# Router weights loaded early, the sample tile projected on four strips of the array, and cache pages gathered in 8 KB rows by GpSimd

## The chip, the cores and the metric

The kernel runs on one core of a Trainium2 chip. A core has a matrix engine (TensorE, PE in the rows; its weight loads are PEld), VectorE (DVE), ScalarE (ACT), GpSimd (POOL) and SyncE (SP), which only issues transfers here. SP, ACT and POOL each have a queue of DMA issues; all of them run on the same 16 DMA engines. The metric is device microseconds (us) from start to end, as the median of several executions. All data is float32.

## The reference, cut to what matters

One decoder layer is computed for 512 prompt tokens and for 8 sample sequences of 4 new tokens (32 tokens), with shared weights:

```
h            = rms_norm(x) @ w_in                      # 1024 -> q,k,v (512 each), hq,f,i,g (512 each), 2 gates (1024 each)
o_sb prompt  = stick-breaking attention over 512 tokens, 8 heads of 64
o_sb sample  = the same over 4096 cached rows per sequence: cache_k[page_table], cache_v[page_table]
               page_table (8, 32) picks pages of 128 rows; a row is 8 heads x 64 floats = 2 KB
o_hg         = HGRN2 recurrence (prompt in chunks; 8 sample states of 64x64 per head are read and written)
x           += (sigmoid(ga) * (o_sb @ w_a) + sigmoid(gb) * (y_b @ w_b)) @ w_out
h2           = rms_norm(x); router: h2 @ w_group (4), h2 @ w_expert (32); top group, top 2 experts of it
x           += sum of weight * expert(h2)              # 32 experts, SwiGLU, 3 matrices of 2 MB each
```

## The kernel before

Each engine has its own program, and semaphores order them. The stages, in TensorE's order, are these.

**Projections and prompt attention (0 to 342 us).** The input projection runs in seven chunks of 512 columns, q, k, v, hq, f, i and g, each a 2 MB weight load. Chunks q, k, hq and g are kept transposed ("cols"). Chunks v, f and i are kept with tokens on the partitions ("rows"): five jobs each, four of 128 prompt rows and a fifth of the 32 sample rows (`project`, L641: 8 steps of the inner dimension, each with 512 moving columns; float32 products appear as two instructions each). ScalarE copies a job out of PSUM (`projection_out`, L1226). q, k and v are projected first (13 jobs), then two jobs of hq. The other jobs are interleaved with the 8 heads of the prompt attention: one between a head's scores (L683) and its remain sums (L693, L697), and one between the remain sums and the next head's scores (two before the remain sums of head 0). The fifth job of f comes after the remain sums of head 2, and the fifth job of i before the remain sums of head 5. ScalarE's and VectorE's softplus chain runs while the first of the two jobs does (ScalarE L1260 to L1266, VectorE L1532 to L1578 for the losses, L1580 to L1583 for the arguments). Before head 0 ScalarE issues one transfer, `lb_logits`.

**Page loop (342 to 754 us).** There are 64 units; a unit is 4 pages of one sequence, 1 MB of keys and 1 MB of values. For unit n TensorE transposes two pages (L766), computes the scores of unit n-1 (L777), transposes the other two, and from n = 7 on (`LAG`) sums the values of unit n-7 (L799). ScalarE (L1338) and VectorE (L1744) copy the transposed keys out of PSUM. After each fourth unit the softplus chain of a set runs on ScalarE and VectorE, and `turn_weights` (L788) transposes the result. From unit 4 to unit 52 every second unit is followed by a part of the HGRN2 recurrence (L821 to L917). Keys and values have rings of three buffers each. The small sample-to-sample products (L736 to L752, `new_rows` semaphore) are placed among the first units.

SP issues the cache loads, one DMA for a page: 128 partitions, 2 KB each (`key_loads` L355, `value_loads` L363). It reads the page numbers into registers first. Its order is keys of n, then values of n-6:

```
for n in range(2, UNITS + LAG - 1):
    if n < UNITS:
        key_loads(n)          # waits: pages of unit n-3 turned
    if n == LAG - 1:
        sp.wait_ge(S("rows_stored"), 64)
        sp.wait_ge(S("new_rows"), 4)
    if n >= LAG - 1:
        value_loads(n - LAG + 1)   # waits: values of unit n-9 summed
```

The weights of the first two branch products (`gate_loads(0)`, 2 MB in 1 KB runs) are issued near the end of this loop at n = 67; `w_branch_a`, `w_branch_b` and `gate_loads(1)` follow after the loop. GpSimd loads the sample states (L530, 16 DMAs), and stores them (L538) when they are done.

**End of the loop (712 to 754 us).** After the scores of unit 63 TensorE sums the values of units 57 to 59, turns the last weights, does `branch_product(0, 0)` (L943), sums units 60 and 61, does `branch_product(0, 1)`, and sums units 62 and 63.

**Branch products (754 to 917 us)**: L943 for the gates and L946 for the two branches.

**Mixing and router (917 to 1020 us).** TensorE multiplies with `w_out`, first the samples (L998: 32 stationary columns, four strips of the output at once), then four prompt tiles (L1005). Between them it transposes the rows (L1019) and computes router logits (`router`, L1031). VectorE first clears a scratch area (L1813) and the router weights (L1814). ScalarE waits for that (`route_zero`), issues the five loads of router weights and biases (L1194) and loads its function table (L1402). VectorE multiplies the router weights with `norm2_w` (L1901) before the first `router`.

**Experts (1020 to 1500 us).** SP streams 6 MB per expert through three buffers. The weights of expert 2 are issued when mixing is done and, in part, when the first gather of rows has landed. GpSimd gathers token rows with an indirect DMA (`rows_in`, L559) and scatters the results (`rows_out`, L567). Then the results are added and stored (until 1520 us).

## Time and profile before

| | us |
|---|---|
| median of 3 runs | 1527.18 (1525.68 to 1533.15) |
| profiled execution, its own time | 1522.24 |
| its span, first to last instruction | 1520.5 |
| TensorE busy | 1339.0 (88%) |
| VectorE, ScalarE, GpSimd busy | 394.6, 353.0, 87.3 |

The profile is of one execution. "Busy" of TensorE includes the fill of its pipeline, so 88% is not 88% of its peak. "PEclk" is the clock granted to TensorE as a share of 2.4 GHz, averaged over a stretch (1.00 is 2.4 GHz, 0.50 is 1.2 GHz). "DMA share" is the mean busy share of the 16 DMA engines; it reads a little over 1 in some stretches. An entry such as `[1.30 <-DMA arena<-in_cache_k]` behind an instruction says that its engine stood idle for 1.30 us before it and what ended that.

### The profile page before, as it was taken

The page shows a single profiled execution, that of the slowest core. Times are in us where ns is not written, and L with a number is a line of the kernel's source. Part 1 is how long each engine was busy: PE and PEld are TensorE (multiplying, and loading weights), DVE is VectorE, ACT ScalarE, POOL GpSimd, SP SyncE. Part 2 cuts the span into 40 slices and gives each one's busy share as a digit, 9 for nine tenths or more (in the row PEclk, how much of TensorE's full clock was granted, in tenths as well). Part 3 has the DMA queues.
Part 4 walks back from the last instruction along what each step waited for, and adds up shares of the span by engine and source line. Part 5 has one row for each costly group of instructions (what it writes and reads, how often), then busy time and mean ns, then how long its engine had stood idle before and what let it go on. Part 6 is the DMA issues. An engine that isn't in the chain of part 4 may idle for free.

```text
span 1520.5 us, 22239 instructions
## 1 busy us (share of the span) xinstructions
PE 1339.0 (88%) x8780; PEld 797.2 (52%) x8780; DVE 394.6 (26%) x723; ACT 353.0 (23%) x566; POOL 87.3 (6%) x144
## 2 busy tenths in 40 slices
PE   7999999978999999787799997969988887888873
PEld 5847544555666667555688883544333332333331
DVE  2012343443444444342011102341111111011103
ACT  2023242424444443564000001110100000000000
POOL 3000000011000000200000000010110101001000
PEclk9999999998999999999899998979999898899987
DMA  6113200018999998999781105049999999999995
GB/s 225 56 56 128 83 0 0 0 45 242 334 358 378 348 344 314 386 383 352 279 321 56 56 25 205 28 158 412 425 426 426 426 426 425 426 426 425 427 392 193
DMA packets 119640, 395.94 MB, mean 260 GB/s; under 512 B 17075, under 2 KB 25284, under 8 KB 107250
## 3 DMA queue, kind: packets, MB, share of 16 engines
q1 hardware_dynamic: 109506, 380.41, 64.5%
q0 software_dynamic: 5984, 11.18, 2.2%
q10 hardware_dynamic: 4048, 2.93, 0.6%
q8 instruction: 71, 1.16, 0.3%
q14 instruction: 31, 0.25, 0.0%
HBM read 386.06 MB, written 16.27 MB: 265 GB/s over the span
## 4 chain that ended last, share of the span: by engine, by line
PE 71%; issue 7%; DVE 6%; DMA 5%; SPq 5%; ACT 4%; ACTq 1%; POOLq 0%; DVEq 0%
PE ps L1118 16%; PE ps L943 8%; PE ps L1141 7%; PE ps L638 7%; PE ps L766 5%; PE ps L641 5%; PE ps L946 4%; PE ps L1005 3%; DMA arena<-in_cache_k 3%; PE ps L777 3%; SPq L363 2%; PE ps L799 2%; SPq L355 2%; PE ps L1129 1%; PE ps L693 1%
## 5 line engine op out<-in xcount | busy, mean ns | idle before, releaser
L1118 PE MATMUL ps<-arena 128*64 128x512 f32 x512 | 252.9, 652 | 68.2 <-issue 66.8
L1119 PE MATMUL ps<-arena 128*64 128x512 f32 x512 | 253.4, 653 | 0.0
L1118 PEld LDWEIGHTS ps<-arena 128*64 128x64 f32 x512 | 74.0, 150 | 212.8 <-issue 210.6
L766 PE MATMUL ps<-ident,arena 128*128 128x128 f32 x1024 | 149.5, 292 | 27.4 <-DMA arena<-in_cache_k 21.4
L766 PEld LDWEIGHTS ps<-ident,arena 128*128 128x128 f32 x1024 | 118.0, 148 | 99.1 <-issue 68.9
L1338 ACT ACTIVATE arena<-ps 128x512 f32<-128x512 f32 x192 | 108.5, 595 | 173.6 <-PE ps L766 173.6
L943 PE MATMUL ps<-mixers,arena 128*128 128x272 f32 x512 | 120.7, 397 | 6.8 <-DMA arena<-in_w_in 6.8
L638 PE MATMUL ps<-mixers,arena 128*128 128x272 f32 x512 | 120.4, 397 | 0.5 <-DVE mixers L1491 0.5
L943 PEld LDWEIGHTS ps<-mixers,arena 128*128 128x128 f32 x512 | 98.2, 192 | 27.8 <-DMA arena<-in_w_in 7.2
L638 PEld LDWEIGHTS ps<-mixers,arena 128*128 128x128 f32 x512 | 97.8, 192 | 21.1 <-DVE mixers L1491 0.6
L641 PE MATMUL ps<-arena,mixers 128*128 128x512 f32 (+1 forms) x240 | 105.4, 594 | 0.0
L1744 DVE COPY arena<-ps 128x512 f32<-128x512 f32 x64 | 44.2, 690 | 178.6 <-PE ps L766 178.5
L1141 PE MATMUL ps<-arena,attn_masks 128*64 128x512 f32 x176 | 81.4, 606 | 0.5 <-DVE attn_masks L1990 0.5
L1142 PE MATMUL ps<-arena,attn_masks 128*64 128x512 f32 x176 | 81.4, 606 | 0.0
L777 PE MATMUL ps<-arena 128*32 128x512 f32 x512 | 75.6, 665 | 0.0
L1119 PEld LDWEIGHTS ps<-arena 128*64 128x64 f32 x512 | 74.0, 150 | 0.0
L799 PE MATMUL ps<-arena 128*32 128x128 f32 x2048 | 69.6, 278 | 3.2 <-DMA arena<-in_cache_v 3.1
L641 PEld LDWEIGHTS ps<-arena,mixers 128*128 128x128 f32 (+1 forms) x240 | 40.9, 174 | 56.6 <-issue 55.8
L1965 DVE TENSOR_TENSOR arena<-ps,arena 128x1024 f32<-128x1024 f32 x16 | 19.6, 1225 | 187.9 <-PE ps L1104 187.7
L799 PEld LDWEIGHTS ps<-arena 128*32 128x32 f32 x2048 | 52.8, 110 | 14.8 <-issue 10.9
L946 PE MATMUL ps<-mixers,arena 128*128 128x272 f32 x256 | 59.8, 392 | 0.0
L1005 PE MATMUL ps<-arena 128*128 128x512 f32 x128 | 59.7, 617 | 0.0
(333 smaller groups left out, 1355.3 us busy)
## 6 DMA issues: line engine op xcount, KB each, us to landing
arena<-in_cache_k SPq DMA_DIRECT2D x256, 256.0 KB, 5.0
arena<-in_cache_v SPq DMA_DIRECT2D x256, 256.0 KB, 5.0
arena<-in_w_gate_exp SPq DMA_DIRECT2D x32, 2048.0 KB, 32.2
arena<-in_w_up_exp SPq DMA_DIRECT2D x32, 2048.0 KB, 37.0
arena<-in_w_down_exp SPq DMA_DIRECT2D x22, 2048.0 KB, 37.7
mixers<-in_w_down_exp SPq DMA_DIRECT2D x10, 2048.0 KB, 37.4
arena<-in_w_in SPq DMA_DIRECT2D x7, 2048.0 KB, 8.6
arena<-in_w_in SPq DMA_DIRECT2D x8, 1024.0 KB, 14.2
```

Source lines behind the costliest of these rows:

```text
L638: last = mm(ps[:, bank + hf, 0:TH], wring[:, c % 3, k, P * j:P * j + P], hT[:, k, TH * hf:TH * hf + TH], start=k == 0, stop=k == KD - 1)
L641: last = mm(ps[0:ROWS[j], bank, :], hT[:, k, P * j:P * j + ROWS[j]], wring[:, c % 3, k, :], start=k == 0, stop=k == KD - 1)
L766: last = turn(ps[:, TURN + j % 2, P * c:P * c + P], kring[n % 3][:, j, P * c:P * c + P], ident[:, :])
L777: last = mm(ps[32 * c:32 * c + 32, ZB, :], qblk_of(m // NGRP, s, c), d_kt[:, n % 2, c, :], start=s == 0, stop=s == PER_SET - 1)
L799: last = mm(ps[32 * c:32 * c + 32, VB, P * s:P * s + P], d_at[:, m % 2, j, 32 * c:32 * c + 32], vring[:, n % 3, j, P * c:P * c + P], start ...
L943: last = mm(ps[:, bank + hf, 0:TH], gw[m // 2 % 2][e][:, k, P * (m % 2):P * (m % 2) + P], hT[:, k, cols], start=k == 0, stop=k == KD - 1)
L946: last = mm(ps[:, bank + hf, 0:TH], wab[e - 2][:, k, P * m:P * m + P], (osbT, ybT)[e - 2][:, k, cols], start=k == 0, stop=k == CT - 1)
L1005: last = mm(ps[:, 2 * (p % 2) + hf, :], mrg[:, k, P * i:P * i + P], wo[k][:, 512 * hf:512 * hf + 512], start=k == 0, stop=k == KD - 1)
L1118: mm(ps[0:BLK, 1 + u, :], own, wgv[w][:, k, :], start=k == 0, stop=k == KD - 1)
L1119: last = mm(ps[BLK:P, 1 + u, :], own, wuv[w][:, k, :], start=k == 0, stop=k == KD - 1)
L1141: mm(ps[0:BLK, 5 + u, :], m_h[:, u, j, :], wdv[w][:, j, 0:512], start=j == 0, stop=j == FJ - 1)
L1338: fn(d_kt[:, n % 2, :, P * j:P * j + P], each(ps[:, TURN + j % 2, :], CT), ACT.Copy).then_inc(S("kT_act"), 1)
```

## The change

There are three parts.

**Router weights.** The five loads of router weights and biases are issued by ScalarE before the attention of head 0, ahead of `lb_logits`, into a tensor of their own that GpSimd clears at the start. `route_zero` no longer stands ahead of them. VectorE's memset of the weights goes.

**Sample tile.** The fifth job of the chunks v, f and i is computed as four matmuls per step instead of one, each with the same 32 stationary columns and 128 of the 512 moving columns, into four strips of 32 output partitions. ScalarE copies the four strips out with four instructions.

**Pages.** GpSimd issues one indirect DMA for the keys of a unit and one for its values. Each partition gets 8 KB, four adjacent rows of a page. The row numbers of all 64 units are computed at the start by VectorE from the page table, which is broadcast to all partitions. Position n of the loop now holds the keys of n and then the values of n-7. The wait for `new_rows` stands before the keys of unit 4; the values of units 0, 1 and 2 are issued at positions 4, 5 and 6. SP is left with the state loads and stores, and issues `gate_loads(0)` and `gate_loads(1)` as soon as the recurrence is done and the branch weights when unit 63 is scored. ScalarE reads and writes the scores of a set in another order of columns (two instructions per set, with a stride), since a buffer's columns no longer follow the order of the cache rows.

```diff
@@ TensorE, project
+                    elif j < 4:
+                        last = mm(ps[:, bank, :], hT[:, k, P * j:P * j + P], wring[:, c % 3, k, :],
+                                  start=k == 0, stop=k == KD - 1)
                     else:
-                        last = mm(ps[0:ROWS[j], bank, :], hT[:, k, P * j:P * j + ROWS[j]], wring[:, c % 3, k, :],
-                                  start=k == 0, stop=k == KD - 1)
+                        for q in range(4):
+                            last = mm(ps[32 * q:32 * q + TS, bank, 0:P], hT[:, k, SEQ:T], wring[:, c % 3, k, P * q:P * q + P],
+                                      start=k == 0, stop=k == KD - 1)
@@ ScalarE, projection_out
+                        for q in range(4):
+                            last = fn(dst[0:TS, j, P * q:P * q + P], ps[32 * q:32 * q + TS, bank, 0:P], func, scale=scale)
@@ GpSimd
+            def unit_loads(n, out, rows, landed):
+                pool.indirect_dma_start(
+                    out=flat(out), out_offset=None, in_=rows,
+                    in_offset=bass.IndirectOffsetOnAxis(ap=unit_i[:, n:n + 1].bitcast(U32), axis=0),
+                    bounds_check=LAST_ROW, oob_is_err=False).then_inc(S(f"{landed}_{n % 3}"), 16)
+            def key_loads(n):
+                if n >= 3:
+                    pool.wait_ge(S("page_turned"), GP * (n - 2))
+                unit_loads(n, kring[n % 3], k_rows, "cache_k")
+            def value_loads(n):
+                if n >= 3:
+                    pool.wait_ge(S("values_summed"), n - 2)
+                unit_loads(n, vring[:, n % 3], v_rows, "cache_v")
+            pool.wait_ge(S("unit_rows"), 1)
+            pool.wait_ge(S("heads_normed"), 2 * CT)
+            key_loads(0)
+            pool.wait_ge(S("attn_weights"), H)
+            key_loads(1)
+            key_loads(2)
             pool.wait_ge(S("attn_values"), H)
             nc.gpsimd.memset(flat(state[:, 0]), 0.0).then_inc(S("states_zero"), 1)
+            key_loads(3)
+            pool.wait_ge(S("rows_stored"), 64)
+            pool.wait_ge(S("new_rows"), 4)
+            for n in range(4, UNITS + LAG):
+                if n < UNITS:
+                    key_loads(n)
+                if n in (4, 5, 6):
+                    value_loads(n - 4)
+                elif n >= LAG + 3:
+                    value_loads(n - LAG)
@@ SP (state loads and stores moved here from GpSimd; cache loads gone)
+            sp.wait_ge(S("yb"), 1)
+            gate_loads(0)
+            gate_loads(1)
             sp.wait_ge(S("unit_scores"), UNITS)
             for e in range(2):
                 sp.dma_start(wab[e], w_br[e]).then_inc(S("w_branches"), 16)
-            gate_loads(1)
@@ ScalarE, order of columns, and router loads moved ahead of lb_logits
-                fn(d_z, ps[:, ZB, :], ACT.Identity, scale=SCALE, bias=d_c[:, 0:1])
+                fn(d_z.rearrange("p (q r) -> p q r", r=GP), ps[:, ZB, :].rearrange("p (r q) -> p q r", r=GP), ACT.Identity, ...)
-            act.wait_ge(S("route_zero"), 1)
-            load(w2c, ...); load(wr[:, :, 0:NG], ...); load(wr[:, :, 8:8 + NE], ...); load(r_b ...) x2
```

## Rows read from the trace of the kernel before

**Rows 1.** The page: span, and busy time of TensorE.

```profile
span 1520.5 us, 22239 instructions
PE 1339.0 (88%) x8780; PEld 797.2 (52%) x8780; DVE 394.6 (26%) x723; ACT 353.0 (23%) x566; POOL 87.3 (6%) x144
```

**Rows 2.** Busy time by stretch, then clock, DMA share and GB/s.

```profile
372.00:600.00 228.00, 222.53 (x3048) 156.80 (x3049) 99.24 (x178) 105.61 (x187) 1.25 (x2) 0.94 0.97 346
...
615.70:711.70 96.00, 77.55 (x988) 51.28 (x988) 34.24 (x47) 54.32 (x87) 9.96 (x16) 0.98 1.05 384
...
753.70:917.00 163.30, 161.72 (x712) 133.72 (x714) 18.73 (x32) 8.72 (x14) 0.00 (x0) 1.00 0.37 131
...
1040.00:1480.00 440.00, 373.17 (x1662) 146.75 (x1663) 53.18 (x84) 35.04 (x59) 43.97 (x44) 0.91 1.01 424
```

**Rows 3.** Waits: from 600 to 715 us, then from 372 to 600 us.

```profile
PE ps L766 <- DMA arena<-in_cache_k: 18.0, 15, 3.8
...
PEld ps L766 <- DMA arena<-in_cache_k: 5.2, 7, 1.5
```

**Rows 4.** Timeline of TensorE, unit 56: start, duration, instructions, idle before.

```profile
673.00 1.09 PE L766 MATMUL ps<-ident,arena 128*128 128x128 f32 x8 [1.30 <-DMA arena<-in_cache_k]
...
676.04 1.08 PE L799 MATMUL ps<-arena 128*32 128x128 f32 x32
678.63 1.09 PE L766 MATMUL ps<-ident,arena 128*128 128x128 f32 x8 [1.51 <-DMA arena<-in_cache_k]
```

**Rows 5.** DMA queues: packets, MB, share of 16 engines' span.

```profile
q1 hardware_dynamic: 109506, 380.41, 64.5%
q0 software_dynamic: 5984, 11.18, 2.2%
```

**Rows 6.** The chain that ended last: start, us, what.

```profile
83.40 34.45 PE ps L641 x80
...
210.03 6.98 PE ps L641 x16
```

**Rows 7.** Timeline: the arguments of head 2, and the strips of L998.

```profile
212.07 0.28 DVE L1583 TENSOR_TENSOR arena<-arena,attn_masks 128x128 f32<-128x128 f32 x1
...
916.75 3.66 PE L998 MATMUL ps<-arena 128*32 128x256 f32 x64 [1.57 <-DVE arena L1811]
```

**Rows 8.** Timeline: head 0, losses done and remain sums begun.

```profile
152.72 0.28 DVE L1578 TENSOR_TENSOR arena<-arena,mask_lt 128x128 f32<-128x128 f32 x1
...
157.63 1.02 PE L693 MATMUL ps<-arena,attn_masks 128*128 128x512 f32 x2
```

**Rows 9.** Timeline: the first units.

```profile
361.46 0.42 DVE L1638 COPY arena<-ps 128x256 f32<-128x256 f32 x1 [0.34 <-PE ps L752]
...
364.81 1.10 PE L766 MATMUL ps<-ident,arena 128*128 128x128 f32 x8 [0.34 <-ACT arena L1338]
```

**Rows 10.** GpSimd's gathers of token rows (tile view).

```profile
L559 POOL DMA_INDIRECT arena<-expert_rows,load_i x16: 988/1042/1190, 1014.5 to 1403.1; - x16
...
DMA to landing us min/median/max: 4.1/12.5/13.2
```

**Rows 11.** Timeline of TensorE at the end of the page loop.

```profile
721.98 1.93 PE L799 MATMUL ps<-arena 128*32 128x128 f32 x32 [3.12 <-DMA arena<-in_cache_v]
723.85 1.12 PE L788 MATMUL ps<-ident,arena 128*128 128x128 f32 x4
731.76 9.31 PE L943 MATMUL ps<-mixers,arena 128*128 128x272 f32 x32 [6.79 <-DMA arena<-in_w_in]
```

**Rows 12.** Timeline around the first router product.

```profile
920.86 4.17 ACTq L1194 DMA_DIRECT2D mixers<-in_w_expert_router  x1
...
925.07 8.37 ACTq L1194 DMA_DIRECT2D arena<-in_b_group_router  x1
...
937.79 1.27 PE L1031 MATMUL ps<-mixers 128*32 128x40 f32 x16 [9.13 <-DVE mixers L1843]
...
939.00 12.77 PE L1005 MATMUL ps<-arena 128*128 128x512 f32 x24
```

138 lines of the change are left out of this document (63 added, 75 removed).

## The prediction

> **What bounds the kernel now.** I read the page first: TensorE is busy 88% of the span and no other engine comes near [rows 1]. It is therefore on the path nearly everywhere, and the question for each stretch is what it waits for. The windows by stretch answer that [rows 2]. From 372 to 600 us (page loop with the recurrence) it is busy 222.5 of 228 us: it is the bound itself. From 615.7 to 711.7 us, in which units 46 to 62 run, it is busy 77.6 of 96.0 us while the DMA engines are full (share 1.05) at 384 GB/s: there the transfers bound it. From 753.7 to 917 us it is the bound again. In the expert stage the DMA engines are full (1.01) at 424 GB/s and TensorE is not. The weights of expert 2 are released by the end of mixing, so the expert stage has a fixed length from there, and whatever is saved ahead of it moves the end one for one.
>
> The list of waits says how much the page loop loses: 18.0 us from 600 to 715 us and at most 5.2 us from 372 to 600 us, all for keys [rows 3]. The timeline of unit 56 shows the pattern: the unit starts 1.30 us late for its keys, its own work runs from 673.00 to 677.12 us, and the next one is 1.51 us late again; 5.63 us between starts [rows 4]. Most units there take 5.42 us with some 4.05 us of work.
>
> **The change part by part.** *Sample tile.* The five jobs of v take 34.45 us in 80 instructions, 6.89 us each, and the fifth is no shorter than the others [rows 6]. The new form is 64 instructions of 128 columns on 32 stationary columns in four strips. Nearest row: `w_out` for the samples has the same 64 on 32 columns in four strips, with 256 columns each, and takes 3.66 us [rows 7]; half of that is 1.8, and the value sums (32 of 128 columns on 32, in 1.08 us [rows 4]) give 2.1. I take 2.0 us. If strips did not overlap, 64 transposes' worth (8 in 1.09 us) would be 8.7 us, a loss of 1.8 a job. The fifth job of v is followed by TensorE's own work: 6.9 - 2.0 = 4.9, less 0.4 for the longer copy-out that the norms wait for, 4.5 us. The fifth job of f stands between the remain sums of head 2 (end 210.03) and the scores of head 3 (217.0) [rows 6]. What is late next is VectorE's last argument, done at 212.35 [rows 7], so 4.6 of its 7 us go. The fifth job of i lies under the softplus chain of head 5: nothing. Sum -9.1 us.
>
> *Router weights, before head 0.* ScalarE is held while it issues these loads. In the present place the third holds it 4.17 us and the fourth 8.37 [rows 12]; with 1.4 for the other three that is 13.9 us, beside 8 MB of other loads. In the new place ScalarE would begin at 136.95 - 4.6 = 132.3 and be free at 146.3 at worst, where head 0's chain wants it at 138.4: 7.9 late. The losses of head 0 are done at 153.0 and the remain sums begin at 157.63 [rows 8], 4.6 us of slack, because two jobs run there. So the cost is between 0 and 3.3 us. The DMA engines stand nearly idle there, so I take 0. The memset and the 12 small instructions for row numbers on VectorE lie under the first four projection jobs, where it idles for 30 us: nothing.
>
> *Router weights, after the branch products.* TensorE stands 9.13 us before the first router product, then runs it (1.27 for about 0.9) and the next 24 instructions in 12.77 us, where 24 at 0.43 us are 10.3: the granted clock had fallen in the wait [rows 12]. All three go: 9.1 + 0.4 + 2.4 = -11.9 us. Next late would be ScalarE's table load and the sums of squares, which end near 925.6; the product can start at 928.66 behind TensorE's own work.
>
> *Start of the page loop.* All this is earlier by 9.1. GpSimd waits for `new_rows` (now 361.88 [rows 9]) before the keys of unit 4; SP waited for it only after the keys of unit 6. The gather is issued at 361.9 and lands after at least 4.1 us [rows 10], plus 1.8 since 1 MB is 0.78 MB more than those gathers move (at 424 GB/s): 367.8 to 369, against a start at 364.81 [rows 9]. The values of unit 0 stand between it and the keys of unit 5. I take +4.5 us; bounds 0 (the lag is caught up in the recurrence) and 8.
>
> *The loop with the recurrence.* TensorE stays the bound: only the waits go, -5 us (bounds 0 and -5.2, plus what the clock gives back).
>
> *Units 46 to 62.* Transfers are the bound, and their rate per run length follows from two rows: 2 KB runs at 384 GB/s and the 16 KB runs of expert weights at 424 [rows 2] give 85 ns and 618 ns on one of 16 engines, so 8.9 ns a run plus 37.2 ns per 1000 bytes; an estimate of 418 GB/s for 8 KB and 349 for 1 KB. When unit 46 starts, the rings are full; 15 units of keys and 14 of values (30.4 MB) must land before unit 63: 72.7 us. The gate weights, 4.2 MB in 1 KB runs that came after the keys before, now fall among them: 12 us. The state stores cost 4 us as before (96.0 less 17 units at 5.42). Together 88.7 against 96.0: -7.3 us. TensorE's own work there is 77.6, so it does not take over.
>
> *End of the loop.* The wait of 6.79 us for gate weights goes, and `branch_product(0, 0)` runs in 7.3 instead of 9.31 us [rows 11], since the gap lowered the clock. Against this, the branch weights now compete with the last values, and the values of unit 59, awaited for 3.12 us now, may be 2 us later. Sum -7 us.
>
> In that last overlap the Trainium skill has a rule (DMA: Bandwidth & Descriptors, section Issuing engines are not separate DMA queues): transfers started by several engines run on the same 16 DMA engines and interleave. The trace agrees: gathers of token rows land in 4.1 us at best and in 12.5 at the median beside SP's full queue [rows 10]. By the rule alone the move to GpSimd would bring no bandwidth; the sum takes its gain from longer runs and an earlier issue, not from the engine.
>
> **The sum.** -9.1 - 11.9 + 4.5 - 5 - 7.3 - 7 = -35.8 us. The profiled execution took 1522.2 (span 1520.5), so 1486.4; the median lies 5 us above it, and the forecast for the median is 1527.2 - 35.8 = 1491 us.
>
> **Rivals.** (A) *The gather's latency replaces the wait.* A key buffer is freed 3.1 us into unit n-3 and needed at the start of n. With a landing of L, a unit takes (L + 3.1) / 3; the 12.5 us of [rows 10] give 5.2 us, about what it is now. Then the page loop gains nothing, and the end keeps -2: 1527.2 - 9.1 - 11.9 + 4.5 - 2 = 1509 us. For it: that median. Against it: SP's queue is nearly empty in this loop. (B) *GpSimd's queue moves less.* Its queue holds 11.18 MB in 2.2% of 16 engines' span (535 engine-us), 334 GB/s against 388 for SP's [rows 5]. At 334 the 120 gathers up to unit 63 (125.8 MB) need 377 us, with gates and states about 399, from 326 on: unit 63 starts at 728 instead of 711.7. +16 - 5 - 11.9 = -1: 1526 us, no change. Against it: those packets are 1.9 KB on average, and short runs cost more.
> The skill's page (DMA: Bandwidth & Descriptors, section Bandwidth) gives 6.15 us, 341 GB/s, for one 1 MB transfer of this kind; by it the time would be that of B. No row here shows a 1 MB transfer from GpSimd, and five or six would be in flight here, which favours the longer transfers of the same table.
> (C) *Slower than before.* GpSimd takes so long to prepare a gather of 128 runs of 8 KB, or the queue is so slow, that a unit takes over 6.4 us (under 328 GB/s, or a landing over 16 us); from there the loop loses 33 us and eats all other gains. At 7 us per unit the loop takes 441 instead of 369: 1527 + 72 - 26 = 1573 us. The 1.04 us that a gather holds GpSimd [rows 10], twice a unit, is far from it, but most of those gathers skip some rows. (D) *TensorE alone bounds the loop*: the gates find room and the first units do not lag: 10 + 4.5 us more, 1477 us.
>
> **How the numbers follow.** Forecast 0.52, A 0.16, B 0.11, C 0.08, D 0.13. The range goes from D with the clock's share (1472) to between A and B: 1520; about 0.2 is left out. A difference under 0.5% (7.6 us) can't be told from none here. Faster by more: the forecast, A and D, 0.81. Within: B, 0.11. Slower: C, 0.08.
>
> **What would show it.** The projection jobs of the sample tile take 2 us and the v jobs together 29.6. The remain sums of head 0 begin at 153 (156 if ScalarE was held). A wait for keys of about 4 us stands before unit 4, and none in the units of the recurrence. In the plain units the starts are 4.9 us apart or less, with DMA near 418 GB/s; at 5.2 with a DMA share well under 1 it is A, with a full share at 334 GB/s it is B. Before `branch_product(0, 0)` no wait for gate weights; before the first router product none either, with the clock at 1.00. The stretch from the first expert product to the end keeps its length. The prediction is wrong if GpSimd's gathers hold it more than 2.5 us each, or if the state loads or gates on SP's queue hold the gathers back for tens of us.

## The result, and where the time went

The changed kernel takes 1509.6 us against 1526.4, a ratio of 0.990 [0.988, 0.993]: 16.8 us less where the forecast said 36. The side was right and the time lies in the range, but less than half of the gain came. Measured twice more beside the experiments, the same file took 1502.1 (0.985 [0.983, 0.987]) and 1512.1 us (0.991 [0.989, 0.993]), while the kernel before stayed between 1523.5 and 1526.4 in the six series that these come from and that follow. The changed kernel has a spread between series that the kernel before does not have, so runs are compared below by their ratio, or within one series. Ratios and their 95% intervals (in square brackets) are of fast executions alone and times are medians of all, which differ by more than 1 us only for the two slowest kernels below (1688.8 us is 1677 by the fast ones, 1651.2 is 1651). A profile is of one execution: "first", "second" and "third" are those of the changed kernel in its three measurements.

The page of the changed kernel (profiled execution 1513.5 us), against [rows 1]:

```profile
span 1511.7 us, 21143 instructions
PE 1336.1 (88%) x8924; PEld 802.6 (53%) x8924; DVE 396.2 (26%) x732; ACT 365.7 (24%) x575; POOL 202.1 (13%) x242
...
q1 hardware_dynamic: 45168, 248.52, 40.6%
q0 software_dynamic: 23328, 143.17, 24.3%
```

Its windows, to be read against [rows 2] (busy time by engine, then clock, DMA share, GB/s):

```profile
372.00:600.00 228.00, 220.73 (x2912) 154.78 (x2912) 93.71 (x163) 108.00 (x181) 71.91 (x70) 0.93 0.85 324
615.70:711.70 96.00, 82.94 (x1048) 54.49 (x1048) 41.10 (x57) 59.88 (x92) 37.76 (x36) 0.95 1.02 400
```

The same two first windows in the profile of the second measurement (span 1497.8 us):

```profile
372.00:600.00 228.00, 224.48 (x3118) 158.85 (x3116) 101.34 (x182) 113.11 (x192) 75.73 (x75) 0.96 0.89 348
615.70:711.70 96.00, 76.92 (x1043) 50.73 (x1045) 38.02 (x53) 58.26 (x89) 33.98 (x33) 0.97 1.03 414
```

In the first 228 us the DMA engines are no longer full (0.85 and 0.89, where it was 0.97), and pages do move faster in the second window (400 and 414 GB/s for 384). What the one profile lacks against the other is matmuls: 2912 against 3118 in the same 228 us. Cut at the starts of fixed pieces of work, read from the timelines (us, and the difference from the kernel before in brackets; each stretch runs from the start of the one piece to the start of the other):

```
stretch                            before   changed, 1st     changed, 2nd     changed, 3rd     forecast
to unit 1                          351.6    344.9 (-6.8)     345.0 (-6.6)     344.9 (-6.7)     -9.1
unit 1 to unit 7                    29.5     36.8 (+7.4)      36.5 (+7.1)      36.7 (+7.2)     +4.5
unit 7 to unit 46 (recurrence)     234.6    240.1 (+5.5)     226.1 (-8.5)     240.0 (+5.4)     -5
unit 46 to unit 63                  96.0     96.4 (+0.4)      90.0 (-6.0)      89.5 (-6.6)     -7.3
unit 63 to branch_product(1, 0)     41.9     38.1 (-3.8)      44.0 (+2.1)      44.4 (+2.4)     -7
to the first gather of rows        260.9    249.0 (-11.8)    249.0 (-11.9)    249.0 (-11.8)    -11.9
to the end                         506.0    506.4 (+0.4)     507.1 (+1.1)     506.8 (+0.9)      0
sum                                         -8.8             -22.7            -9.3             -35.8
```

The sums are the differences of the spans. The router term (the sixth row) holds to the tenth. The fourth and fifth rows trade with each other: together they are -3.4, -4.0 and -4.1 us where the forecast has -14.3, and this is the one large miss that all three profiles share. Four rows of the timeline show the others: the strips, the head after them, unit 4, and the router product.

```profile
110.94 1.95 PE L648 MATMUL ps<-arena,mixers 128*32 128x128 f32 x64
...
268.00 2.08 PE L700 MATMUL ps<-arena,attn_masks 128*128 128x512 f32 x2 [5.96 <-DVE arena L1605]
...
362.71 1.54 PE L773 MATMUL ps<-ident,arena 128*128 128x128 f32 x6 [4.59 <-DMA arena<-in_cache_k,arena]
...
931.22 0.76 PE L1038 MATMUL ps<-router_w,mixers 128*32 128x40 f32 x16
```

A sample tile takes 1.95 us (2.0 forecast). In front of the remain sums of head 5 the shorter i tile leaves TensorE 5.96 us of idle time, and the sums then start at 2.08 us where the same two matmuls take 1.13 in the run with the i tile in one strip. Unit 4 waits 4.59 us for its keys. The router product follows the work before it without a wait and takes 0.76 us instead of 1.27 [rows 12].

What the fourth and fifth rows have to move can be read from the DMA queues. From unit 46 to unit 63 the pages' queue carried this much (packets, MB, share of 16 engines' time): in the kernel before (615.7 to 711.7 us), in the first profile (621.8 to 718.2), in the second (607.7 to 697.7), and in the run with late gates below (613.2 to 701.8).

```profile
q1 hardware_dynamic: 19575, 35.64, 101.0%
q0 software_dynamic: 4859, 35.39, 89.5%
q0 software_dynamic: 4856, 35.32, 94.2%
q0 software_dynamic: 4868, 35.45, 95.6%
```

It is the same in all four, within 0.4 MB of 34 loads of 1.05 MB (35.65 MB): 17 of keys and 17 of values. The sum had 29 (30.4 MB), because it took both rings for full at the start of unit 46. They aren't. In the second profile the gathers for the keys of units 47 and 48 are issued 3.7 and 0.2 us before unit 46 starts, and a gather of keys takes 7.9 us to land (median in the recurrence):

```profile
603.98 1.06 POOL L509 DMA_INDIRECT arena<-in_cache_k,arena  x1 [0.30 <-issue]
607.55 0.98 POOL L509 DMA_INDIRECT arena<-in_cache_k,arena  x1 [1.18 <-PE ps L773]
607.70 1.24 PE L773 MATMUL ps<-ident,arena 128*128 128x128 f32 x8
```

By the landing events of that trace the keys of unit 47 are there at 613.20, and unit 47 starts at 613.35: the ring holds what is on its way, not what has landed.

At the end of the loop (against [rows 11]), first profile, then second:

```profile
724.01 1.08 PE L806 MATMUL ps<-arena 128*32 128x128 f32 x32 [0.79 <-DMA arena<-in_cache_v,arena]
727.51 1.08 PE L806 MATMUL ps<-arena 128*32 128x128 f32 x32 [2.42 <-DMA arena<-in_cache_v,arena]
731.72 1.93 PE L806 MATMUL ps<-arena 128*32 128x128 f32 x32 [3.13 <-DMA arena<-in_cache_v,arena]
```

```profile
703.56 1.08 PE L806 MATMUL ps<-arena 128*32 128x128 f32 x32 [0.80 <-DMA arena<-in_cache_v,arena]
707.03 1.93 PE L806 MATMUL ps<-arena 128*32 128x128 f32 x32 [2.39 <-DMA arena<-in_cache_v,arena]
711.38 1.93 PE L806 MATMUL ps<-arena 128*32 128x128 f32 x32 [2.41 <-DMA arena<-in_cache_v,arena]
717.88 10.05 PE L950 MATMUL ps<-mixers,arena 128*128 128x272 f32 x32 [3.53 <-DMA arena<-in_w_in]
```

The wait of 6.79 us for gate weights has turned into waits for the last values, 6.3 us in three pieces where 3.1 stood before; in the second profile they are 5.6, and 3.5 us for gate weights stand there as well. What became of the early gate weights is in SyncE's queue (start, time that the issues hold SyncE; first profile, then second):

```profile
623.70 38.74 SPq L356 DMA_DIRECT2D new_hgrn_sample<-arena  x16
674.89 47.08 SPq L362 DMA_DIRECT2D arena<-in_w_in  x4
```

```profile
609.64 51.38 SPq L356 DMA_DIRECT2D new_hgrn_sample<-arena  x16
661.07 53.36 SPq L362 DMA_DIRECT2D arena<-in_w_in  x4
714.47 5.92 SPq L369 DMA_DIRECT2D arena<-in_w_branch_a  x1
```

The state stores, which GpSimd had issued in 10 us before, hold SyncE for 38.7 and 51.4 us. They stand in front of the gate loads but hardly delay them: the gate loads also wait for the recurrence (`yb`), whose last piece VectorE finishes at 674.9 in the first profile, 12 us after the stores are through, and at 656.7 in the second, 4.4 us before the gate loads begin (5.1 in the third). What is slow is the gate loads themselves, which hold SyncE for 47.1 and 53.4 us beside GpSimd's gathers. So in the second profile the branch weights, meant for the end of unit 63's scores, are asked for at 714.5, and the gates are in only at 717.9. In the first no gate is waited for, and rows four and five of the table together are no better for it.

### The profile page after: what moved, and what is told of

The parts are those of the page before. It is cut to its first block, busy times and chain, and to the rows that moved or that the text cites. A ratio compares the mean times of both kernels' runs of the same rounds, so it can differ in the third digit from the quotient of the medians.

```text
span 1511.7 us, 21143 instructions
## 1 busy us (share of the span) xinstructions
PE 1336.1 (88%) x8924; PEld 802.6 (53%) x8924; DVE 396.2 (26%) x732; ACT 365.7 (24%) x575; POOL 202.1 (13%) x242
## 4 chain that ended last, share of the span: by engine, by line
PE 77%; issue 6%; DVE 6%; DMA 5%; ACT 4%; ACTq 0%; SPq 0%; POOLq 0%; DVEq 0%
PE ps L1125 16%; PE ps L773 7%; PE ps L950 7%; PE ps L1148 7%; PE ps L641 7%; PE ps L953 4%; PE ps L1012 4%; PE ps L644 4%; PE ps L784 3%; PE ps L806 3%; DMA arena<-in_cache_k,arena 3%; PE ps L700 1%; PE ps L1136 1%; PE ps L690 1%; PE ps L704 1%
## 5 line engine op out<-in xcount | busy, mean ns | idle before, releaser
L773 PE MATMUL ps<-ident,arena 128*128 128x128 f32 x1024 | 156.9, 298 | 22.3 <-DMA arena<-in_cache_k,arena 13.4
L773 PEld LDWEIGHTS ps<-ident,arena 128*128 128x128 f32 x1024 | 121.1, 151 | 97.1 <-issue 74.2
L509 POOL DMA_INDIRECT arena<-in_cache_k,arena x64 | 66.0, 1032 | 530.4 <-PE ps L773 218.2
L1771 DVE COPY arena<-ps 128x512 f32<-128x512 f32 x64 | 44.2, 690 | 188.5 <-PE ps L773 188.4
L644 PE MATMUL ps<-arena,mixers 128*128 128x512 f32 x192 | 84.3, 594 | 0.0
L509 POOL DMA_INDIRECT arena<-in_cache_v,arena x64 | 68.9, 1076 | 63.2 <-PE ps L806 42.1
L1990 DVE TENSOR_TENSOR arena<-ps,router_w 128x1024 f32<-128x1024 f32 x16 | 19.6, 1225 | 191.8 <-PE ps L1111 191.7
```

Source lines behind the costliest of these rows:

```text
L509: pool.indirect_dma_start(out=flat(out), out_offset=None, in_=rows, in_offset=bass.IndirectOffsetOnAxis(ap=unit_i[:, n:n + 1].bitcast(U32) ...
L644: last = mm(ps[:, bank, :], hT[:, k, P * j:P * j + P], wring[:, c % 3, k, :], start=k == 0, stop=k == KD - 1)
L773: last = turn(ps[:, TURN + j % 2, P * c:P * c + P], kring[n % 3][:, j, P * c:P * c + P], ident[:, :])
```

## Experiments

Eighteen runs in five series (four kernels in each of the first four, two in the fifth), each series on one chip beside the kernel before.

### The parts alone

Router weights early, everything else as before:

> The kernel before with the early router weights alone. If that term of the sum is right, TensorE no longer stands 9.1 us before the first router product and runs the next 24 instructions at the full clock: 1526.4 - 11.9 = 1514.5 us, and the losses of head 0 on VectorE are done before its remain sums are called for, so the first page is transposed at 342.5 us as before. If ScalarE's hold delays head 0, up to 3.3 us less gain. If the expert stage gives the time back (it starts earlier but is bound by something else), about 1526 us.

1514.3 us, 0.993 [0.991, 0.995]: -11.7 us, as forecast. One sign missed: the first page is transposed at 345.9 us in its profile, not at 342.5. ScalarE is not the reason. The five loads hold it 0.3 to 0.7 us each, and it is free at 140.9, before the scores of head 0 begin (141.03). These follow the same wait of 1.42 us as before, but then the granted clock is 0.58 from 141 to 148 us and they take 3.66 us for 2.42:

```profile
141.03 3.66 PE L683 MATMUL ps<-arena 64*128 64x512 f32 x8 [1.42 <-DVE arena L1528]
```

A single profile can thus be 2 to 3 us off here: of the runs below, two (keys ahead of the wait, late gates) start unit 1 at 347.4 and 347.3 us, where the changed kernel, with the same code up to there, starts it at 344.9 three times. Router and strips, pages as before:

> The changed kernel with the page part undone: SP loads the pages in its old order and runs of 2 KB; early router weights and four strips stay. Theory 1 (the page part costs time, the other two parts give what was forecast less some 2 us): 1526.4 - 11.9 - 7 = 1507.5 us, no slower than the changed kernel's 1509.6, with units 1 to 46 in 264 us instead of 277. Rival (the page part gains and one of the others has failed): 1515 to 1523 us.

1503.7 us, 0.985 [0.981, 0.990]. Those two parts alone give as much as the whole change. Unit 1 starts at 343.0 us, 8.6 before that of the kernel before, and units 1 to 46 take 262.7 us (264 expected). Beside the changed kernel on one chip (series 4):

> The changed kernel with the page part undone (2 KB runs from SyncE), again, now beside the changed kernel itself: 1503.7 us in its first series, 0.985 of the kernel before. What the page part is worth is this run less the first of this call. Theory (the page part gains some 10 us in the recurrence and in units 46 to 62 and gives back 7 at unit 4 and 3 to 6 at the end of the loop): the two within 4 us where the signs are absent; where they are there, this kernel, which gathers nothing in the loop, keeps 1504 us and the changed one takes 1510.

1510.1 us, 0.990 [0.988, 0.992], against 1512.1, 0.991 [0.989, 0.993]. The page part as built is worth nothing that can be told; it is a sum of gains and losses. The expectation that this kernel keeps 1504 us failed: it is 6 us slower than in its first series too, though its profile has none of the pauses told of below. The gain can be seen in one place. From unit 46 to `branch_product(1, 0)` the three kernels with 2 KB pages from SyncE and early router weights or strips take 139.5 to 140.0 us (the kernel before 138.0), the changed kernel 133.8 to 134.5.

### The wait at unit 4

```diff
             key_loads(3)
+            key_loads(4)
+            key_loads(5)
             pool.wait_ge(S("rows_stored"), 64)
             pool.wait_ge(S("new_rows"), 4)
             for n in range(4, UNITS + LAG):
-                if n < UNITS:
+                if 6 <= n < UNITS:
                     key_loads(n)
```

> The changed kernel with the keys of units 4 and 5 gathered before GpSimd waits for new_rows. Theory 1: the lag at unit 4 (13.1 us for that unit instead of 6.6) comes from the queue behind that wait and goes wholly: -6.5 us, 1503 us. Rival: the recurrence and the last units are bound by transfers, which start no earlier on the whole, so that waits for keys appear later instead: 1508 to 1510 us.

1495.2 us, 0.981 [0.977, 0.985]. What is left of the wait, behind unit 6's first pages, is shorter:

```profile
372.05 1.09 PE L775 MATMUL ps<-ident,arena 128*128 128x128 f32 x8 [2.81 <-DMA arena<-in_cache_k,arena]
```

Unit 4 takes 6.58 us again instead of 13.1, and units 1 to 7 take 31.1 us instead of 36.5. That is 5.4 us by the profile, near the 6.5 of theory 1; the 1503 us expected had started from the slow measurement (1509.6). The ratio stands 0.4% (6 us) below the changed kernel's in series 2 and 1% below its other two; the intervals overlap with that of series 2 alone. There is no unedited kernel in this run's own series.

### The changed kernel again

> The changed kernel once more, nothing edited, as the base of this series. Its first profile took 283.3 us from the start of unit 7 to the start of unit 53, where the kernel with late gate loads, which is the same code up to there, took 267.4. If that stretch really depends on the code outside it, it takes 283 again. If it varies from execution to execution, it takes 267 to 275 here, and the wait of 4 to 5 us for keys before unit 4, with a second unit at half clock behind it, is there in both. Time: 1509 us (1505 to 1514).

1502.1 us. Units 7 to 53 do not need 283 us: the second expectation held. A third time:

> The changed kernel a third time, nothing edited, beside three others on one chip. So far it took 1509.6 us and 1502.1. In the slower of the two profiles the units with a recurrence step take 0.2 to 1.0 us longer each and units 57 to 62 5.6 to 5.97 us instead of 5.0 to 5.8. The two runs with the stores behind the weights (1510.8 and 1499.4 us) show the same two signs. Theory (it comes with the chip or the hour and is the same for all kernels of one call that gather with GpSimd): this run and the next show the same signs, either both or neither. Rival (it comes with an edit): this one 1502 us and without them, whatever the next one shows.

1512.1 us. Of the two signs of the first profile it has one, the longer units with a recurrence step; units 57 to 62 take 5.1 to 6.1 us, most of them 5.1. The three-edits kernel beside it shows the same sign, as the theory said. Waits of TensorE from 386 to 600 us in the third profile, then in the second:

```profile
PE ps L773 <- ACT arena L1356: 2.2, 5, 0.6
PE ps L850 <- PE ps L850: 1.7, 3, 0.6
PE ps L924 <- issue: 1.4, 1, 1.4
PE ps L850 <- issue: 0.9, 1, 0.9
```

```profile
PE ps L773 <- ACT arena L1356: 1.0, 3, 0.3
PE ps L924 <- issue: 0.3, 1, 0.3
```

In the slower profiles TensorE pauses inside runs of short matmuls (L850, L924) with no data outstanding, some 4 us in all in the first, and more of the stretch runs at half clock: from 372 to 600 us the granted clock averages 0.93 in the first and third profile and 0.96 in the second, which is some 7 us of work (an estimate: 0.03 of 228 us). It goes with the series and not with an edit: the run with stores moved (series 3, below) shows 9.6, 6.9 and 10.5 us for units 16, 18 and 24, the unedited kernel of series 4 9.6, 6.9 and 10.3, and the one of series 2 8.6, 6.1 and 8.6. It is worth 10 us from unit 7 to 38 (188.5 against 178.8). It needs the gathers too: with the pages from SyncE, in series 4, the profile has no such pause. What sets it was not found. Instruction fetches alone don't: one of 16 KB, about 1 us long, lies beside each of the three pauses in L850 of the first profile, but the second has fetches at the same places without a pause.

### The exp and the i tile

```diff
-                fn(d_e.rearrange("p (r q) -> p r q", r=GP), d_z.rearrange("p (q r) -> p r q", r=GP), ACT.Exp
+                fn(d_e, d_z, ACT.Exp)
...
-                    last = turn(ps[:, WB, P * j:P * j + P], d_e[:, P * j:P * j + P], ident[:, :])
+                    last = turn(ps[:, WB, P * j:P * j + P], d_e.rearrange("p (q r) -> p r q", r=GP)[:, j, :], ident[:, :])
```

> The changed kernel, but the last exp of each set (16 of them) reads its argument in order, and the transposes that turn the weights read every fourth column instead. In the changed kernel's profile that exp takes 1156 ns where the kernel before takes 625, and the sums of the next unit wait 0.33 us for it once a set, in the stretch where TensorE is the bound. Theory (the strided read on ScalarE lengthens the path): exp back to about 630 ns, the waits of 0.3 us gone, 8 to 16 times 0.33, that is 3 to 5 us less than the changed kernel. Rival 1 (the transposes pay for the stride in its place): the four transposes of a set take over 0.8 us instead of about 0.55, and the time is as before within 2 us. Rival 2 (not on the path): exp short, time unchanged.

1503.3 us, 0.985 [0.983, 0.988], against 1502.1: rival 2. The exp of the changed kernel, then of this one (page groups, mean ns last):

```profile
L1378 ACT ACTIVATE arena<-arena 128x512 f32<-128x512 f32 x16 | 18.5, 1156 | 8.4 <-DVE arena L1786 8.4
```

```profile
L1378 ACT ACTIVATE arena<-arena 128x512 f32<-128x512 f32 x16 | 10.0, 626 | 7.1 <-DVE arena L1785 7.1
```

Units 14, 22 and 30 are 0.33 us shorter each, as expected, but the sum of such pieces, some 2 us (an estimate), is below what the times tell. With this, the keys edit and the i tile back in one strip (`elif j < 4 or CHUNKS[c][1] is itok`, in one matmul of 512 columns per k):

> The changed kernel with three edits: the keys of units 4 and 5 asked for ahead of GpSimd's wait for the new rows (this edit alone was worth 14 us), the exp of each set read in order as in the run above, and the sample tile of the i projection in one strip again (6.9 us of work under the softplus chain of head 5, instead of 2 us). Theory: these add, 1495 - 4 - 2 = 1489 us; the remain sums of head 5 run at the full clock (1.13 us for the first group instead of 2.08) and the page loop starts 2 us earlier against the heads. Rival: the i tile was hidden only in part, and its 5 us come back in full: 1494 us.

1489.1 us, 0.978 [0.975, 0.981]; in series 4 and 5 again:

> The kernel with three edits (keys of units 4 and 5 ahead of GpSimd's wait, exp in order, i tile in one strip) again: 1489 us in its first series, 13 us below the changed kernel beside it. Theory: the three edits act in stretches of their own, so 11 to 14 us below the run before, whatever level that has.

> The kernel with three edits, nothing else, as the base of the run before on the same chip: 1489 or 1505 us, by the level that its chip has; in both cases 1 to 2% below the kernel before.

1505.1 (0.987 [0.985, 0.989]) and 1494.6 us (0.979 [0.976, 0.982]). The gain over the unedited kernel beside it was 13 us in series 2 and 7 in series 4, below the 11 to 14 expected there. 1494.6 is neither of the two levels of the last expectation: from unit 7 to 38 the three profiles take 174.8, 188.2 and 182.6 us, so it is a spread and not two levels. The timeline of the first run, in series 2, shows head 5 at the full clock, without the long gap:

```profile
266.69 1.13 PE L702 MATMUL ps<-arena,attn_masks 128*128 128x512 f32 x2 [0.85 <-DVE arena L1606]
```

This is the fastest version, below both kernels wherever it stood beside them.

### Weights and stores in SyncE's queue

All gates behind the keys, alone and with the keys edit:

```diff
             sp.wait_ge(S("yb"), 1)
+            sp.wait_ge(S("page_turned"), GP * (UNITS - 2))
             gate_loads(0)
-            gate_loads(1)
             sp.wait_ge(S("unit_scores"), UNITS)
+            sp.wait_ge(S("values_summed"), UNITS - 3)
...
+            gate_loads(1)
```

> The changed kernel with the gate and branch weights issued as late as before (the first pair when the keys of the last unit have been issued, the rest after the last values). Theory G (4.2 MB of gate weights among the last units is what keeps them at 5.8 us each): units 58 to 63 take 5 us each, unit 63 starts about 8 us earlier, and the end of the loop gives 5 of it back: 1506 us. Rival (the gather itself can't do better): units as now, and the end of the loop 5 us longer: 1515 us.

> The changed kernel with the keys of units 4 and 5 asked for ahead of GpSimd's wait, and the gate and branch weights, 6.2 MB in 1 KB and longer runs, issued behind the keys instead of in the middle of them. Theory (the early gate loads took transfer time from units 46 to 62, and each edit acts in its own stretch): units 58 to 62 5.2 us each instead of up to 7, but a wait comes back before the branch products; alone the late gates were worth 4 us, so 1495 - 4 = 1491 us. Rival (with the first edit the rings are fuller when the gates come, so that their cost is hidden already and only the new wait before the branch products counts): 1495 us or up to 5 more.

1505.4 us (0.988 [0.983, 0.992]) and 1498.4 (0.984 [0.981, 0.986]). Units 58 to 61 fall to 5.1 to 5.3 us each in both, as theory G said, and its 1506 us is met. But the wait for the first gates is 5.2 us again, and from unit 46 to `branch_product(1, 0)` the first takes 134.2 us, as the unedited kernel does (133.8 to 134.5). For the second the rival held. The state stores moved behind all of these weights:

> The changed kernel, with one edit: SyncE stores the 16 pieces of sample states (1 MB in 256-byte runs, 4096 packets) behind the gate and branch weights, not ahead of them. In the changed kernel those stores hold SyncE 51.4 us from 609.6 on, and the 4 gate loads behind them (4096 packets of 1 KB) another 53.4, so that the branch weights are asked for at 714.5 and the first branch product waits 3.5 us for its gate weights. Theory (the stores stand in SyncE's queue, and a packet of it takes its turn beside GpSimd's 8 KB packets whatever its length): the gate loads hold SyncE again some 50 us, now from about 610, and are there by 665; the branch weights go at 697; no wait for gate weights; units 47 to 62 0.2 us shorter each, since the stores' packets are gone from that stretch. Sum 3.5 + 2 (clock after the wait) + 2 = 7 us off the changed kernel's 1502: 1495 us. Rival (what the loads give up, the values take): the branch weights, asked for 17 us earlier, land on the last values and their waits grow from 5.6 to 10 us: 1502 us.

1510.8 us, 0.991 [0.988, 0.994], in a series without an unedited kernel; the unedited one of series 4, with the same long units, has 0.991 too. The gates came in time and the 7 us did not come. The theory had the gate loads start at about 610 us; they started at 669.4, when the recurrence was done, and in the changed kernel's three profiles the stores ahead of them had delayed them by 0, 4.4 and 5.1 us only. From unit 46 to `branch_product(1, 0)` its profile takes 131.5 us, 2 to 3 less than the unedited kernel's three, and the whole time doesn't show it. With the three edits:

> The four edits together: keys of units 4 and 5 ahead of GpSimd's wait, the exp read in order, the i tile in one strip, the stores of states behind the weights. The first three gave 1489 us, 0.978 of the kernel before. Theory (the last acts by itself): 5 to 7 us less, 1483 us. Rival (in the kernel with three edits the first branch product no longer waited for gate weights, the values of the last units do): 1489 us, with the wait for values at 6 us or more.

1499.4 us, 0.984 [0.980, 0.987], with 5.6 us of waits for the last values. There is no run of three edits beside it; the one of series 4, with the same long units, has 0.987 [0.985, 0.989], so no gain can be told. Last, only the first gates early, with the page loop otherwise free of weights:

> The kernel with three edits, and of the weights for the branch products only the first gates (2.1 MB) are asked for in the page loop; the branch weights (4.2 MB) and the second gates (2.1 MB) wait until the values of unit 60 are summed. In the kernel with three edits the last values are awaited 5.7 us and the loop from unit 63 to the third branch product takes 33 to 38 us, beside 4.2 MB of gates and 4.2 of branch weights on their way. Theory (weights asked for early take the place of the last pages, 2.1 MB is 5 us at 413 GB/s, 4.2 is 10): units 57 to 62 at most 5.2 us each, the waits for the last values down from 5.7 to 2 us, the first gates in time, no wait for the branch weights: 5 to 8 us below the run beside this one. Rival (as with all gates late: what the values gain, the weights lose, since the second gates or the branch weights are now late by as much): within 2 us of the run beside it, with a wait for weights of 3 us or more among the branch products.

1496.6 us (0.980 [0.977, 0.983]) beside 1494.6: the rival, though its other sign, 3 us or more for weights among the branch products, did not show (2.5). The last values are still awaited 6.1 us (0.8, 1.9 and 3.5; 5.7 in the run beside it) and the first gates 2.5 (3.2):

```profile
710.76 1.08 PE L809 MATMUL ps<-arena 128*32 128x128 f32 x32 [1.89 <-DMA arena<-in_cache_v,arena]
715.29 1.94 PE L809 MATMUL ps<-arena 128*32 128x128 f32 x32 [3.45 <-DMA arena<-in_cache_v,arena]
720.78 10.06 PE L953 MATMUL ps<-mixers,arena 128*128 128x272 f32 x32 [2.49 <-DMA arena<-in_w_in]
```

with its queue of SyncE:

```profile
612.37 51.33 SPq L356 DMA_DIRECT2D new_hgrn_sample<-arena  x16
663.74 28.78 SPq L362 DMA_DIRECT2D arena<-in_w_in  x2
```

So the branch weights and second gates do not take the last values' time: without them the waits are as long. While these values are awaited the DMA engines are full (share 1.03 from 702 to 716 us in this run, 387 to 396 GB/s). That the values, which run 7 units behind the keys, are simply the last bytes through full DMA engines fits all five runs, but no run took bytes away from the pages, and it is argued, not shown.

### Run length, queue or place

Pages from SyncE, but in 8 KB runs, each page on 32 neighbouring partitions:

```diff
-  sp.dma_start(kring[n % 3][:, j, :], a["cache_k"][0, bass.ds(page, 1)].rearrange("a s h d -> (a s) (h d)")
+  sp.dma_start(flat(kring[n % 3])[32 * j:32 * j + 32, :], ....rearrange("a (i r) h d -> (a i) (r h d)", r=GP)
```

> The pages again from SyncE in the order of the kernel before (early router weights and strips kept, states stored by GpSimd), but each page laid over 32 partitions, so that a run is 8 KB instead of 2. The same with 2 KB runs took 1503.7 us, 0.985 of the kernel before. Theory (run length carries the gain in the loop, and the issuing engine does not): the waits for keys in the recurrence go (5 us), units 54 to 61 take 5.15 us or less instead of 5.42 and the DMA engines move over 400 GB/s instead of 373 from 616 to 712 us; no wait of 4 us before unit 4, the gate weights still ask for theirs at the end: 1503.7 - 5 - 5 = 1494 us. Rival 1 (the order, keys ahead of values, carries it): units at 5.4 us and 1503 us; the next run falls instead. Rival 2 (GpSimd's own queue carries it): both this and the next run stay at 1503 us. The 16 stores of states, 256-byte runs from GpSimd beside pages in 8 KB runs, hold GpSimd 10 us as in the kernel before if short packets suffer only on SyncE's queue, and 40 to 51 us if it is short packets beside long ones.

> As the run before, but also in the changed kernel's order: values 7 units behind the keys instead of 6, and their first three together. Theory (run length): 1494 us, within 3 us of the run before, since the order only moves which of two full rings is filled first. Rival (order): 5 us or more below the run before.

1688.8 us (1.100 [1.093, 1.107]) and 1651.2 (1.085 [1.080, 1.089]). Both times missed all that was expected. The order keys ahead of values is worth some 26 us where transfers are slow (1677 against 1651). Only the stores did as expected, 10.0 us from GpSimd. Windows of the first:

```profile
372.00:600.00 228.00, 169.01 (x2031) 115.95 (x2030) 66.18 (x115) 78.25 (x131) 0.00 (x0) 0.88 1.02 246
616.00:712.00 96.00, 72.96 (x919) 50.18 (x921) 29.47 (x55) 30.27 (x52) 1.25 (x2) 0.82 0.99 221
```

The DMA engines are fully busy and move 246 GB/s. Then the same with `[j:P:GP, :]` in place of `[32 * j:32 * j + 32, :]`, so that a page's 32 runs lie on every fourth partition:

> Pages from SyncE in 8 KB runs again, but the 32 runs of a page lie on every fourth partition over all 128, instead of on 32 neighbouring ones. The positions of a unit come in another order, so the outputs are not the reference's; the work is the same. With 32 neighbours the loop moved 246 GB/s at a full DMA share, against 348 to 385 with 2 KB runs, and the kernel took 1689 us. Theory (the runs of one page crowd onto a few of the ways into SBUF): spread, a page lands in 5 us as with 2 KB runs instead of 10.6 to 12.7, units 54 to 61 take 5.15 us, and the kernel 1494 us. Rival (32 long runs from SyncE are slow by themselves, whatever partitions they go to, 2 for each of 16 engines): 1650 to 1690 us again.

1529.6 us, 1.003 [1.002, 1.005] (one of its twelve executions took 3333 us and is not in the ratio): about 147 us less than with neighbours (1677), from the place alone. So the theory's mechanism held, and its time missed by 36 us. A page lands in 4.2 us at the median (12.4 and 14.1 with neighbours; 5.1 and 5.2 with 2 KB runs), and the windows read:

```profile
372.00:600.00 228.00, 214.38 (x3022) 153.23 (x3023) 96.16 (x175) 107.12 (x181) 1.25 (x2) 0.96 0.94 334
616.00:712.00 96.00, 74.87 (x907) 49.43 (x909) 32.65 (x44) 51.06 (x78) 9.96 (x16) 0.93 0.96 348
```

It is still some 20 us above 2 KB runs from SyncE (1503.7 and 1510.1), and above GpSimd's gathers of the same 8 KB runs. Long runs are therefore not what speeds the loop up: on SyncE's queue they moved less (348 GB/s) than short ones (376 in the same window, same series). One gather of 128 runs, which covers all partitions at once, moves 400 to 414.

The Trainium skill has a rule that fits the 246 GB/s (SBUF — State Buffer, section Door 1: The DMA port swizzle): what a transfer moves depends on how many of SBUF's 16 ports its partitions reach, and +32 stays on the same port. By its formula 32 neighbours reach eight ports and every fourth partition all sixteen. The traces agree in kind, 246 GB/s against 334.

## Why the prediction was wrong, step by step

The step that failed is the sentence "When unit 46 starts, the rings are full; 15 units of keys and 14 of values (30.4 MB) must land before unit 63". The runs showed 17 and 17 (35.3 to 35.6 MB) in its place, with the kernel before no less than with the changed one. The second miss, in two of three series, is the recurrence, and its cause is open.

**Strips: -6.7 for -9.1.** A job takes 1.95 us. The tiles of v and f gave what was forecast, as the remain sums of head 5 begin 9.4 us earlier than before (268.0 against 277.4). The step "the fifth job of i lies under the softplus chain of head 5: nothing" failed: that job had kept TensorE busy in a gap that VectorE sets, the gap grew to 5.96 us, and the sums behind it began at half the clock and took 2.0 us more (granted clock 0.69 from 268 to 274.7 us); the last head's value sums took 0.6 more. With that job long again, unit 1 starts at 341.1 us in one profile, 10.5 before the kernel before; the two repetitions have 343.9 and 340.9.

**Router weights: right, -11.8.** Head 0's chain was not held up by ScalarE's loads, and the router product had no wait. The bound of 13.9 us for that hold was far off: the five loads took 2.8 us.

**Start of the page loop: +7.2 for +4.5.** The wait at unit 4 was seen and priced right (4.6, 4.3 and 4.4 us). What was left out is that the clock falls in it, so that the work behind it takes longer (six transposes in 1.54 us, where eight take 1.09 at the full clock). Two lines of code undo most of it.

**The recurrence: -8.5 or +5.4 for -5.** The waits for keys went in all three profiles (none from 386 to 600 us). In the second profile the term is as forecast and a little more. In the first and third, pauses within TensorE's own instruction stream and more time at half clock take it back and more. This is 10 us of the miss in those series, and its cause stays open. The ScalarE exp on every fourth column, 1156 ns for 625, is visible in it, with 2 us at most.

**Units 46 to 62 and the end of the loop: together -3.4 to -4.1 for -14.3.** These are two terms of the sum but one count of bytes. The rate was right: 418 GB/s was estimated, and 411 to 418 are moved between units 46 and 63 in the second and third profile. The count was not. A buffer that has been asked for is not a buffer that has landed, and with 34 loads instead of 29 the sum has 12.5 us more (5.2 MB at 418 GB/s), so that the two terms come to -1.8 us instead of -14.3. The rest of the sum holds: the stretch takes 88.7 us in the run without early gates, where 34 loads and the 4 us of stores make 89.3. With early gates the same bytes pass in another order. In the second profile the gates hardly move before unit 63 (1.7 MB beside the pages, 1.05 of it states), so units 46 to 62 gain 6 us and the end loses 2; in the first it is the other way round. From unit 46 to `branch_product(1, 0)` all three profiles move 52.8 to 52.9 MB.

Two more steps of the end term failed. It took away the wait for gate weights and put 2 us for the values in its place; the last values were awaited 6.3 us instead of 3.1, and in the second and third profile 3.5 and 4.0 us for gates came back. And it took the gate loads for quick to issue, where they hold SyncE 47 to 53 us. Gates late, stores late, or weights late each moved the wait from one tile to another, with no gain that the times show.

The reason given for the rate, "longer runs", fell as well: 8 KB runs from SyncE were slower than 2 KB ones. Which property of the gather gives its rate (all partitions in one transfer, or the queue) was not separated further.

Of the rivals, A's total (1509) matches by luck, and not its mechanism: gathers of keys land in 7.9 us at the median in the recurrence, which by A's formula allows 3.7 us a unit. B's 334 GB/s and C's slow gathers did not occur; a gather holds GpSimd 0.99 us at the median, a single one 3.6 us. B's unit 63 at 728 should read 725 (326 and 399). D's zero for the first units was had by the keys edit. The plain units were forecast at 4.9 us or less; units 58 to 62 take 5.0 to 6.1 us in the three profiles, with full DMA engines.

## What to carry to other kernels

Where transfers bound a loop, count the loads that land between two points of it: in a steady ring they are as many as the units between them, and buffers still on their way are no stock. When a load is moved ahead in a queue, look at what it waits for besides the queue, and at how long issuing it takes beside full queues. When a short piece of work under a long wait is made shorter, look at the clock of what follows the wait, not only at the path. And before long runs are credited with a gain, see how many partitions one transfer covers; then measure a changed kernel in more than one series, since it may vary where the old one does not.

## What the runs showed of the hardware

- Beside GpSimd's 8 KB gathers, at a DMA share of 1.02 to 1.03, SyncE was held 38.7 us (first profile) and 51.4 us (second and third) by 16 stores of 1 MB in all (4096 runs of 256 bytes), 42.6 to 53.4 us by 4 loads of 4.2 MB (4096 runs of 1 KB), and 28.8 us by half of those: 9.5 to 14 ns a run, for short and longer runs alike. The Trainium skill says (DMA: Bandwidth & Descriptors, section Queues, rings and completion order) that each DMA engine takes turns between its queues packet by packet; that 1 and 4.2 MB take about as long agrees with it. The reverse case does not look like it: the same stores from GpSimd beside SyncE's pages held GpSimd 10 us and landed in 5.1 us at the median beside 2 KB runs, in 4.9 beside spread 8 KB runs, against 29.7 us from SyncE (the kernel with three edits).
- The same 8 KB runs from the same queue moved 246 GB/s onto 32 neighbouring partitions and 334 onto every fourth, at a DMA share of 1.02 and 0.94.
- A ScalarE exp over 512 columns of SBUF takes 1156 ns reading every fourth element, 626 in order. The strided read from PSUM costs nothing (684 ns, 683 before), and TensorE's transposes on strided columns hardly anything (292 ns, 286 in the changed kernel); their weight loads take 206 ns for 146, under the matmuls.
- The same program can differ by 14 us in one stretch between series (240.1 and 226.1 us), through pauses in runs of short matmuls and more time at half clock.
